# Two of the last four expert weight pieces loaded as sixteen eight-partition transfers each

## What is computed

```
def expert_block(args):
    tok, e = args
    xb = xt[tok]
    return (jax.nn.silu(xb @ w_gate[e]) * (xb @ w_up[e])) @ w_down[e]
...
contrib = y_rows[pos] * gates[:, None]
y = jax.ops.segment_sum(contrib, flat_tok, num_segments=n_tok)
```

## Time and profile before

| what | value |
|---|---|
| median of 3 runs | 1380.4 us (1380.16 to 1381.01) |
| the profiled execution's own time | 1378.5 us |
| its span, first to last instruction | 1376.7 us |
| granted TensorE clock, mean over the span | 0.997 |
| PE busy | 96% of the span |
| DMA queue of the loads (q1) | 433.27 MB, 81.1% of 16 engines' span |

### The profile page before, as it was taken

One profiled execution on the slowest core, in us unless ns is written; L12 is line 12 of the kernel. 1 busy time (PEld: TensorE's weight loads), 2 busy tenths in 40 slices (PEclk: granted clock), 3 DMA queues, 4 the chain that ended last, 5 costly groups with the idle time before them and its releaser, 6 DMA issues.

```text
span 1376.7 us, 31861 instructions
## 1 busy us (share of the span) xinstructions
PE 1326.5 (96%) x14177; PEld 796.7 (58%) x14177; DVE 439.6 (32%) x759; ACT 325.8 (24%) x526; POOL 30.1 (2%) x42
## 2 busy tenths in 40 slices
PE   6999999999999999999979999999999999999975
PEld 6987888888898974354333353354354345345332
DVE  4656655555578672201101101101101100110102
ACT  4645545544556842000000000000000000000001
POOL 2000000000011300000000000000000000000000
PEclk9999999999999999999999999999999999999998
DMA  9733555555453458999999999999999999999994
GB/s 293 273 123 127 194 184 186 196 195 188 127 164 123 153 217 335 374 413 418 413 412 419 414 410 420 415 410 419 416 408 419 416 395 418 417 401 417 418 408 187
DMA packets 133038, 438.34 MB, mean 318 GB/s; under 512 B 10690, under 2 KB 64160, under 8 KB 116512
## 3 DMA queue, kind: packets, MB, share of 16 engines
q1 hardware_dynamic: 131824, 433.27, 81.1%
q0 software_dynamic: 1072, 2.98, 0.7%
HBM read 435.18 MB, written 1.05 MB: 317 GB/s over the span
## 4 chain that ended last, share of the span: by engine, by line
PE 87%; DMA 7%; DVE 3%; SPq 2%; issue 1%; ACT 1%; POOL 0%; DVEq 0%
PE bank L1388 37%; PE bank L1409 16%; PE bank L1153 7%; PE bank L903 6%; PE bank L905 5%; PE bank L904 5%; DMA ring<-in_moe_w_down 4%; PE bank L1154 4%; DMA ring<-in_moe_w_gate 1%; DMA raw<-in_ev_w_in 1%; SPq L799 1%; PE bank L1440 1%; PE bank L1156 1%; PE bank L1460 1%; DVE arena L2170 0%
## 5 line engine op out<-in xcount | busy, mean ns | idle before, releaser
L1388 PE MATMUL bank<-ring,arena 128*32 128x512 f32 (+1 forms) x5632 | 537.3, 540 | 4.4 <-DMA ring<-in_moe_w_up 3.1
L1388 PEld LDWEIGHTS bank<-ring,arena 128*32 128x32 f32 x5632 | 179.6, 110 | 340.5 <-issue 323.6
L1409 PE MATMUL bank<-ring,arena 128*32 128x256 f32 x4928 | 272.4, 379 | 16.7 <-DMA ring<-in_moe_w_down 15.6
L1409 PEld LDWEIGHTS bank<-ring,arena 128*32 128x32 f32 x4928 | 158.2, 110 | 131.3 <-DMA ring<-in_moe_w_down 23.3
L702 DVE TENSOR_TENSOR low<-raw,high 128x2048 fp32r<-128x2048 f32 x73 | 167.3, 2294 | 83.5 <-ACT high L697 83.4
L697 ACT ACTIVATE high<-raw 128x2048 fp32r<-128x2048 f32 x73 | 139.3, 1910 | 53.3 <-PE bank L905 43.4
L1153 PE MATMUL bank<-ht_both,high 128*128 128x512 f32 x392 | 140.6, 398 | 0.6 <-DVE ht_both L1929 0.6
L2477 DVE TENSOR_TENSOR expert_rows<-expert_rows,bank 128x512 f32<-128x512 f32 (+1 forms) x44 | 27.3, 621 | 317.0 <-issue 163.0
L1154 PE MATMUL bank<-ht_both,low 128*128 128x256 f32 x448 | 116.6, 281 | 0.0
L1816 ACT ACTIVATE expert_rows<-bank 128x512 f32<-128x512 f32 (+1 forms) x44 | 23.7, 544 | 388.6 <-PE bank L1388 388.6
L1827 ACT ACTIVATE y_h<-bank 128x256 fp32r<-128x256 f32 x22 | 8.4, 383 | 396.8 <-PE bank L1409 396.8
(11 more groups left out here) (328 smaller groups left out, 1169.1 us busy)
## 6 DMA issues: line engine op xcount, KB each, us to landing
ring<-in_moe_w_down SPq DMA_DIRECT2D x112, 1024.0 KB, 18.7
ring<-in_moe_w_gate SPq DMA_DIRECT2D x64, 1024.0 KB, 19.4
ring<-in_moe_w_up SPq DMA_DIRECT2D x64, 1024.0 KB, 23.2
ring<-in_moe_w_gate SPq DMA_DIRECT2D x64, 768.0 KB, 20.8
ring<-in_moe_w_up SPq DMA_DIRECT2D x64, 768.0 KB, 20.6
raw<-in_ffn_w_gate SPq DMA_DIRECT2D x14, 1024.0 KB, 5.0
raw<-in_ffn_w_up SPq DMA_DIRECT2D x14, 1024.0 KB, 5.0
raw<-in_ffn_w_down SPq DMA_DIRECT2D x14, 1024.0 KB, 4.9
```

The costliest lines, as they stand in the source:

```text
L1388: ins = mm(ps(use)[q * GRP:(q + 1) * GRP, 0:width], rows[:, k, r * GRP:(r + 1) * GRP], weights[:, q, :, :], start=k == 0, stop=k == DK - 1)
L1409: ins = mm(ps(use)[q * GRP:(q + 1) * GRP, 0:DN], m_act_t[:, r, first + c, :], ring[:, at + c * DM + q * DN:at + c * DM + (q + 1) * DN], st ...
```

## The change

In the last sorted item, pieces 42 and 43 (both down pieces; four pieces, 42 to 45, are the last four) are not loaded by one transfer of 128 partitions each, but by sixteen transfers of eight partitions each. Each of these is 64 KB, sixteen rows of 4 KB, and adds 16 to the piece's semaphore, so the piece adds 256. `expert_landed` raises the count that TensorE waits for by the 240 more, for piece 42 and 43 of that item and for whatever uses the same two semaphores afterwards. The waits for the places in the ring stay as they are, one for each piece, ahead of its first transfer. Nothing else changes: the same bytes go to the same places, and pieces 44 and 45 follow on the same queue.

```
+EIGHTHS = 8
+NARROW = (EXPERT_PIECES - 4, EXPERT_PIECES - 3)
...
         def expert_landed(j, item):
-            return expert_full[j % FULLS], 16 * (j // FULLS + 1) + item * (16 * EXPERT_PIECES // FULLS)
+            full = 16 * (j // FULLS + 1) + item * (16 * EXPERT_PIECES // FULLS)
+            for narrow in NARROW:
+                if j % FULLS == narrow % FULLS and (item, j) >= (NE - 1, narrow):
+                    full += 16 * (P // EIGHTHS - 1)
+            return expert_full[j % FULLS], full
...
                 for j in range(FIRST_TURN, EXPERT_PIECES):
                     wait_expert_used(sp, held_before(j), item)
-                    load_expert(wt, j)
+                    if item == NE - 1 and j in NARROW:
+                        dst, src = expert_piece(wt[EXPERT_ORDER[j][0]], j)
+                        for p in range(0, P, EIGHTHS):
+                            sp.dma_start(dst[p:p + EIGHTHS], src[p:p + EIGHTHS]).then_inc(expert_full[j % FULLS], 16)
+                    else:
+                        load_expert(wt, j)
```

## The result

The change makes the kernel slower: 1393.86 us, median of four runs (1392.79 to 1396.72), against 1380.28 us for the kernel before (four runs, 1380.09 to 1381.01). The ratio is 1.0101, with a 95% interval of 1.0083 to 1.0118. The profiled execution took 1394.32 us and has a span of 1392.5 us, 15.8 us more than before's, at a granted clock of 0.987 (before: 0.997). The forecast was 1379.2 us with a range up to 1387.6; the result lies outside it.

The account below looks back on a forecast made before the run. The expert weights' DMA stream, ended by its late engines, was taken as the bound. Piece 45 would start 0.3 us (first issue held) to 1.9 us earlier; the middle, 1.1 to 1.2 us, gave 1379.2 us, range 1377.2 to 1387.6.

Parts of the forecast that it names:

- The stream sets the end, and a late engine each landing: Last down pieces: TensorE waits for each piece's bytes until the last DMA engine brings its share; late engines trail by 8.5 to 12 us.
- Pieces 40 and 41 are untouched: Whole pieces queued ahead of the small transfers keep their times; piece 41 still starts on TensorE at 1352.87.
- the floor of TensorE: Back-to-back down pieces after piece 41 let piece 45 start no earlier than 1359.6 to 1360.6, capping the gain at 2.1 to 3.1 us.
- 32 x 0.159 = 5.1 us: Time of one small-transfer piece on the eight engines used: 32 rows each at 0.159 us, in place of 2.55 us.
- The small pieces use the early half: Pieces 42 and 43 fall on the eight early engines, ending near 1355.6; the late half ends 5.1 us sooner; weighted 3 to 1.
- the first rival: Small transfers fall on the late half of the engines: 5.1 to 7.5 us more, 1385.5 to 1387.9 us; chance 0.22.
- Pieces 44 and 45 land 4.9 us after their issue and one piece later: Behind the small issues, 44 lands 4.9 us after issue, at 1359.9 or 1358.3; 45 follows 2.5 us behind.
- The price of an issue: SP's cost for each of the 32 small issues, address work included: 0.56 us, bounds 0.44 to 0.94 us.
- the fourth rival: Small issues are cheap, 0.44 to 0.5 us, so TensorE is the bound: 2.1 to 3.1 us faster, 1377.3 to 1378.3; chance 0.22.
- a hold beyond the first issue: Sign of a wrong prediction: the full queue holds small issues after the first; only the first was allowed a hold, to 1337.36.
- the second: Rival: small issues cost 0.67 to 0.94 us, making the kernel about 3 to 11.4 us slower, 1383.4 to 1391.8; chance 0.11.
- The small transfers one behind the other: Pieces 42 and 43: at the skill's 0.95 us for 64 KB, the 32 transfers without overlap would take 30 us.

Follow-up runs that it names:

- the quiet queue: The changed kernel, but SP waits until piece 41 has landed before it issues the first small transfer: 1403.6 us, ratio 1.0164.
- e8_extra: Against the kernel before: pieces 42 and 43 whole, each followed by eight additional eight-partition transfers into every fourth partition of 0 to 63: 1383.54 us, ratio 1.0018.
- e11_upper: As the kernel with additional transfers behind whole pieces 42 and 43, but these write partitions 64 to 127 and read the matching rows: 1394.88 us, ratio 1.0102.
- e7_eight_columns: Against the kernel before: pieces 42 and 43 as eight transfers each, of all 128 partitions and 256 columns: 1380.91 us, ratio 1.0008.

## Why the prediction was wrong

**What happened.** What the runs show is that the place in SBUF matters: loss of 2.3 us in the lower half against 14.1 in the upper; halves of 64 partitions against slices of columns, 1389.7 against 1380.9 us; the memory side exchanged with no effect clear of noise. My reading of it is this. Each engine writes the rows of a whole piece to partitions of its own, so all ways into SBUF are used evenly. The six early engines that a small transfer reaches come to it first, near 1344, and write to partitions whose ways the late engines need for pieces 38 to 41. Both slow down: 213 GB/s at a share of 0.90, the late engines some 4.6 us a piece in place of 2.6. After that the small transfers slow each other, as in the quiet queue, 76 GB/s for eight engines. In the kernel with halves all engines are busy and move 224 to 226 GB/s, a little over half of 408, into half of the partitions. No view shows a way or names an engine; that the early ones write into the ways of the late ones is read from e8_extra and e11_upper together.

The Trainium skill (SBUF — State Buffer, "Door 1: The DMA port swizzle (why [64,N] ≈ [32,N])") says that four neighbouring partitions and the four that lie 32 further on share one of sixteen ports. Eight neighbours would be on two ports, every sixteenth partition of 128 on four, every fourth within 32 on eight, and 64 partitions of a half on eight. The runs agree in the order: the first two collapsed (213 and 185 GB/s), the third much less (307, then 208 at a share of 0.69), the fourth ran at half rate. How many ports were in use at a time they don't show, since transfers overlap: sixteen neighbours are four ports by this rule, and the kernel with them moved 202 to 226 GB/s, as much as the one with halves and their eight. The Trainium skill (DMA: Bandwidth & Descriptors, "The descriptor swizzle") gives each engine of a 128-partition transfer one port, the low eight engines those of partitions 0 to 63; e8_extra, which by this rule kept each engine to its own port, and e11_upper, which didn't, agree. The prediction asked what a small transfer does to the engines, and not what it does on the side of SBUF.

**By its steps.**

*The stream sets the end, and a late engine each landing:* right. The chain still ends in a transfer and TensorE's last pieces, and near the end two late engines are alone at work (share 0.14, then 0.08; piece 45's last two increments at 1375.7 and 1378.4).

*"Pieces 40 and 41 are untouched":* this is the step that failed. The prediction took them to be out of reach because they were queued first. They came 5.5 and 6.6 us late net of the offset, held back by transfers behind them in the queue, and took the floor of TensorE (1359.6 to 1360.6) with them.

*"32 x 0.159 = 5.1 us" a piece on the eight engines:* also wrong, for the same reason. An engine's pace with a 128-partition transfer was taken for its pace with any. The six early engines took some 10 us for piece 42 (they were done with piece 41 from 1343.9 to 1345.5, and with 42 at 1354.8), and in the quiet queue the piece took 14.9 us.

*The small pieces use the early half:* true for six of the eight engines. The two late ones bring pieces 42 and 43 last (32 of 128 increments each, up to 1368.1 and 1373.4). The run with twice the load and little crowding shows what the eight engines' additional rows cost by themselves: 2.3 us, where all on the early half would be nothing and the first rival asked for 5.1. The increments fit two late engines that aren't the last of all. Before, all late engines but the last two had piece 45 by 1360.4; 5.1 us more makes 1365.5, 2.8 us behind the straggler's 1362.7. The straggler with 5.1 us more would have been at 1367.8. In the run the last increment comes at 1368.0, or 1365.4 net of its profile's offset of 2.6 us. This is an estimate from the groups, as no increment names its engine. That a small transfer reaches eight engines is right: 0.51 in the quiet queue, and nine increments a transfer.

*Pieces 44 and 45 land 4.9 us after their issue and one piece later:* nearly right for fourteen engines, which had piece 44 5.3 to 6.3 us after its issue at 1360.60. TensorE needs all sixteen, and the two late ones were still in the small pieces: 15.3 and 17.2 us from issue to landing.

*The price of an issue:* inside its bounds, and cheaper than taken. 0.277 + 0.19 = 0.46 us where nothing is awaited, for 0.56 taken and 0.44 as the lower bound. The first one was not held (0.35 us). Both of these pointed to the fourth rival's gain of 2.1 to 3.1 us, and were worth nothing: 32 issues took 22 us, for they waited on a queue that drained at half speed. The prediction had named a hold beyond the first issue as a sign of being wrong, and had put no price on it.

*The rivals.* None had the mechanism. The far end of the second, 1391.8 us, is nearest to the result, but issues were cheap, not dear, and with cheap ones it asked for a gain. The first gave the right sign with the wrong price: of its 5.1 to 7.5 us the load is 2.3 (e8_extra) and the ends are nothing (e7_eight_columns). The range went to its upper end and no further, because every bound was made of counts of rows at one speed. The signs that the prediction gave were useful nevertheless: pieces 40 and 41 later than 9.3 and 11.8 us behind piece 37 (14.6 and 18.2) said at once that the fault lay ahead of the small pieces.

*The small transfers one behind the other.* The estimate from the Trainium skill's 0.95 us for 64 KB (DMA: Bandwidth & Descriptors, "Bandwidth", a row for transfers over 128 partitions that GpSimd issues) was 30 us for the 32. The quiet queue took 29, of which 0.93 us each for piece 42. That the two agree is luck as far as the runs show: it isn't overhead of small transfers that slowed these, since sixteen of 128 KB over all partitions cost nothing.

*What stays open.* How much of the 13.6 us is slowing of whole pieces and how much is small pieces slowing each other I can only read off the timeline (6.6 and 6.1 us), not separate: one piece alone cost 5.4 us. Which ways were in use, and why every fourth partition still lost a quarter of the rate from 1348 to 1352, no view shows. Why eight engines are ahead is open too. Whether small transfers with every fourth partition, own ways only and cheap issues could gain anything wasn't tried; no kernel here was faster than the kernel before.

## What to carry to other kernels

If a load has to be split, split it by columns and leave it at 128 partitions. In a full queue a transfer over a part of the partitions slowed not only itself but whole transfers ahead of it, in every kernel here that sent such transfers there, but for the one that kept to the lower half. By my reading work can't be moved from late DMA engines to early ones this way, since the rows keep their partitions and so their way into SBUF. And read the DMA share and the rate together: here a share of 0.9 with half of the usual GB/s was contention, a share of 0.5 with half the GB/s idle engines.

## What was not expected of the hardware

- Two transfers of 64 partitions for one of 128 nearly halved the rate of everything under way (253 GB/s already from 1340 to 1344 in its profile) and cost 4.9 us a piece, where sixteen of eight partitions cost 6.8.
- The issue of a transfer with eight stepped partitions takes SP 0.61 us (every sixteenth) to 0.70 us (every fourth); with eight neighbours 0.277 us, with 128 partitions 0.367 us. The stepping counts on the side of SBUF alone: every sixteenth row of memory into neighbours is 0.277 us.
- In the profile before, eight engines were ahead of the rest by 8.5 us at the end of a stream that gave every engine the same bytes; doubling the rows of eight engines in the last two pieces, six of them early and two late, cost 2.3 us only.
